# Assigning experts for two of five token tiles during the mixed stage of a transformer layer with a mixture of experts

## The reference, cut to what matters

```python
g_idx   = argmax(softmax(xt @ router_grp_w + router_grp_b))           # 1 of 4 groups
e_logit = (xt @ router_exp_w + router_exp_b).reshape(-1, 4, 4)[.., g_idx]
top_w, top_i = top_k(softmax(e_logit), 2)                             # 2 of its 4 experts
combine = sum(one_hot(g_idx * 4 + top_i) * g_w * top_w / sum(top_w))
out     = sum_e combine[:, e] * (silu(xt @ w_gate[e]) * (xt @ w_up[e])) @ w_down[e]
```

## Time and profile before

| what | value |
|---|---|
| median of 3 runs | 767.57 us (767.41 to 770.96) |
| the profiled execution | 768.89 us |
| its span in the trace | 767.2 us |
| mean granted TensorE clock | 0.974 of full |
| PE, VectorE, ScalarE, GpSimd busy | 714.9, 535.2, 406.7, 108.8 us |

### The profile page before, as it was taken

How to read it: one execution, slowest core, us unless ns; L and a number is a source line. 1 busy time by engine, 2 the same in 40 slices (tenths; PEclk the granted TensorE clock), 3 DMA queues, 4 the chain that set the end, 5 groups by cost and what they waited for, 6 DMA issues and landing times.

```text
span 767.2 us, 10726 instructions
## 1 busy us (share of the span) xinstructions
PE 714.9 (93%) x3858; PEld 538.7 (70%) x3858; DVE 535.2 (70%) x834; ACT 406.7 (53%) x615; POOL 108.8 (14%) x164
## 2 busy tenths in 40 slices
PE   4899999999999989999999389999999999999985
PEld 1359998939989855555554268888888888888753
DVE  5355616369442016667556889999999999999968
ACT  1645523330233015455543467887888878888713
POOL 2000000000031006654221101111111111111000
PEclk9999999999999999999999689999999999999998
DMA  9992235113358649800013899999999999999943
GB/s 323 418 390 109 94 126 220 33 78 124 138 106 213 271 139 398 234 1 30 1 51 131 285 371 387 372 369 385 373 381 392 381 369 379 373 363 366 330 190 137
DMA packets 81905, 188.55 MB, mean 246 GB/s; under 512 B 9092, under 2 KB 19492, under 8 KB 78532
## 3 DMA queue, kind: packets, MB, share of 16 engines
q1 hardware_dynamic: 73652, 168.93, 60.1%
q0 software_dynamic: 6448, 16.86, 6.6%
q10 hardware_dynamic: 1760, 2.17, 0.9%
HBM read 175.46 MB, written 18.38 MB: 253 GB/s over the span
## 4 chain that ended last, share of the span: by engine, by line
PE 86%; DVE 7%; DMA 2%; ACT 2%; issue 1%; SPq 0%; ACTq 0%; POOLq 0%; DVEq 0%
PE bank L1936 55%; PE bank L1838 15%; PE bank L1847 5%; PE bank L1858 3%; PE bank L2087 2%; PE bank L1888 1%; DMA big<-y_scratch 1%; PE bank L2065 1%; PE bank L2058 1%; DVE big L1800 1%; DVE big L1810 1%; DVE big L1256 1%; DVE big L1805 1%; DMA big<-h_scratch,big 1%; PE bank L1873 1%
## 5 line engine op out<-in xcount | busy, mean ns | idle before, releaser
L1651 DVE TENSOR_TENSOR WL<-slot,WH 128x1024 fp32r<-128x1024 f32 x188 | 219.1, 1221 | 9.4 <-ACT WH L1143 8.2
L1143 ACT CAST WH<-slot 128x1024 fp32r<-128x1024 f32 x188 | 183.5, 1057 | 2.4 <-PE bank L1936 1.4
L1936 PE MATMUL bank<-WH,xgTh 128*128 128x512 f32 x256 | 102.4, 400 | 3.0 <-DVE xgTl L1643 3.0
L1936 PE MATMUL bank<-WH,xgTl 128*128 128x512 f32 x256 | 100.7, 393 | 0.0
L1936 PE MATMUL bank<-hTh,WP 128*128 128x384 f32 (+1 forms) x320 | 99.2, 310 | 0.6 <-DVE hTl L1301 0.6
L1936 PE MATMUL bank<-hTh,WL 128*128 128x384 f32 (+1 forms) x320 | 98.7, 308 | 0.0
L1936 PE MATMUL bank<-hTl,WP 128*128 128x384 f32 (+1 forms) x320 | 98.7, 308 | 0.0
L1936 PE MATMUL bank<-WL,xgTh 128*128 128x512 f32 x248 | 96.5, 389 | 0.0
L1838 PE MATMUL bank<-slot,big 128*128 128x512 f32 (+1 forms) x224 | 87.7, 539 | 0.1
L541 DVE TENSOR_TENSOR WL<-slot,WP 128x1024 fp32r<-128x1024 f32 x24 | 29.5, 1247 | 62.0 <-ACT WP L535 61.6
L1847 PE MATMUL bank<-ident,big 128*128 128x128 f32 x424 | 60.9, 284 | 7.5 <-DMA big<-h_scratch,big 5.3
(11 more groups left out here) (265 smaller groups left out, 1079.8 us busy)
## 6 DMA issues: line engine op xcount, KB each, us to landing
slot<-in_w_up SPq DMA_DIRECT2D x16, 2048.0 KB, 17.9
slot<-in_w_down SPq DMA_DIRECT2D x16, 2048.0 KB, 16.7
slot<-in_w_gate SPq DMA_DIRECT2D x15, 2048.0 KB, 15.7
slot<-in_w_ada SPq DMA_DIRECT2D x12, 2048.0 KB, 13.1
slot<-in_w_in SPq DMA_DIRECT2D x6, 2048.0 KB, 18.9
y_scratch<-dftp SPq DMA_DIRECT2D x1, 5120.0 KB, 40.4
big<-y_scratch SPq DMA_DIRECT2D x10, 512.0 KB, 10.2
slot<-in_w_out SPq DMA_DIRECT2D x2, 2048.0 KB, 15.4
```

Source lines behind the costliest of these rows:

```text
L1143: act.copy(WH[:, high_half(w, s), r, :], quarter(n, s, w, r)).then_inc(high_ok[w], 1)
L1651: dve.tensor_tensor(quarter_low(n, s, w, r), quarter(n, s, w, r), WH[:, high_half(w, s), r, :].bitcast(F32), ALU.subtract).then_inc(low_ok ...
L1936: ins = pe.matmul(out, l[u], r[v], start=first and i == 0, stop=last and i == 2)
```

## The change

The code from `first_max` to line 1606 becomes a function `assign(tiles)` on a range of tiles. It is called twice: for tiles 0 and 1 at the end of step 19, behind `weighted` of ("wa", 3, 0), and for tiles 2 to 4 where the code was. PE waits for `assigned` to reach 2 before the ranks. The tables, their places and their numbers stay the same.

```diff
+EARLY_ASSIGNED, EARLY_TILES = 19, 2
...
+            def first_max(val, mx, out, sets):
+
+                n = sets.stop - sets.start
+                link(dve.tensor_reduce(mx[:, sets], val[:, sets], AX, ALU.max))
+                link(dve.tensor_tensor(out[:, sets], val[:, sets], mx[:, sets].broadcast_to([P, n, NG]), ALU.is_equal))
+                link(dve.scalar_tensor_tensor(out=keys[:, sets], in0=out[:, sets], scalar=-float(NG),
+                                              in1=iota[:, 0:NG].unsqueeze(1).broadcast_to([P, n, NG]),
+                                              op0=ALU.mult, op1=ALU.add))
+                link(dve.tensor_reduce(low[:, sets], keys[:, sets], AX, ALU.min))
+                link(dve.tensor_tensor(out[:, sets], keys[:, sets], low[:, sets].broadcast_to([P, n, NG]), ALU.is_equal))
+
+            def assign(tiles):
+
+                sets = slice(tiles.start * SETS, tiles.stop * SETS)
+                first_max(lsets, max1, flat1, sets)
+                link(dve.scalar_tensor_tensor(out=rest_val[:, sets], in0=flat1[:, sets], scalar=-1.0e30, in1=lsets[:, sets],
+                                              op0=ALU.mult, op1=ALU.add))
+                first_max(rest_val, max2, flat2, sets)
+                link(dve.tensor_tensor(by_group(either[:, tiles]), experts1[:, tiles], experts2[:, tiles], ALU.add))
+                dve.tensor_tensor(by_group(A[:, tiles, :]), by_group(either[:, tiles]), in_group(tiles), ALU.mult)\
+                   .then_inc(assigned, 1)
+                n = tiles.stop - tiles.start
+                link(dve.tensor_tensor(by_group(A2[:, tiles]), experts2[:, tiles], in_group(tiles), ALU.mult))
+                link(dve.scalar_tensor_tensor(out=choice[:, 0, tiles], in0=A2[:, tiles], scalar=float(TOK),
+                                              in1=tid[:, tiles].unsqueeze(2).broadcast_to([P, n, NE]),
+                                              op0=ALU.mult, op1=ALU.add))
...
                 if v in LOGITS_AT:
                     logits(LOGITS_AT[v])
+                if v == EARLY_ASSIGNED:
+                    have(dve, "rt", EARLY_TILES - 1)
+                    dve.wait_ge(tm_ok, CT * H)
+                    assign(slice(0, EARLY_TILES))
             have(dve, "rt", NT - 1)
...
-            first_max(lsets, max1, flat1)
-            link(dve.scalar_tensor_tensor(out=rest_val, in0=flat1, scalar=-1.0e30, in1=lsets, op0=ALU.mult, op1=ALU.add))
-            first_max(rest_val, max2, flat2)
...
-            link(dve.tensor_tensor(by_group(either), experts1, experts2, ALU.add))
-            dve.tensor_tensor(by_group(A[:, :, :]), by_group(either), in_group, ALU.mult).then_inc(assigned, 1)
-            link(dve.tensor_tensor(by_group(A2), experts2, in_group, ALU.mult))
+            assign(slice(EARLY_TILES, NT))
...
-            pe.wait_ge(assigned, 1)
+            pe.wait_ge(assigned, 2)
```

More of the change, by code:

```diff
@@ L1520, in weighted, with by_group, in_group @@
                     dve.tensor_tensor(x[:, b, cols], x[:, b, cols], w, ALU.add).then_inc(x1_ok, 1)
+            flat1, flat2 = (v.rearrange("p t g j -> p (t g) j") for v in (first_of, second_of))
+            experts1, experts2 = first_of[:, :, 1:SETS, :], second_of[:, :, 1:SETS, :]
+            def by_group(v):
+                return v.rearrange("p t (g j) -> p t g j", j=EPG)
+            def in_group(tiles):
+                n = tiles.stop - tiles.start
+                return first_of[:, tiles, 0, :].unsqueeze(3).broadcast_to([P, n, NG, EPG])
@@ L1577, in _ @@
                     logits(LOGITS_AT[v])
+                if v == EARLY_ASSIGNED:
+                    have(dve, "rt", EARLY_TILES - 1)
+                    dve.wait_ge(tm_ok, CT * H)
+                    assign(slice(0, EARLY_TILES))
             have(dve, "rt", NT - 1)
[L1580 to L1590, removed]
-            first_max(lsets, max1, flat1)
-            link(dve.scalar_tensor_tensor(out=rest_val, in0=flat1, scalar=-1.0e30, in1=lsets, op0=ALU.mult, op1=ALU.add))
-            first_max(rest_val, max2, flat2)
[L1594 to L1598, removed]
-            link(dve.tensor_tensor(by_group(either), experts1, experts2, ALU.add))
-            dve.tensor_tensor(by_group(A[:, :, :]), by_group(either), in_group, ALU.mult).then_inc(assigned, 1)
-            link(dve.tensor_tensor(by_group(A2), experts2, in_group, ALU.mult))
+            assign(slice(EARLY_TILES, NT))
             def choices(c):
                 return choice[:, c]
-            link(dve.scalar_tensor_tensor(out=choices(0), in0=A2, scalar=float(TOK),
-                                          in1=tid[:, :].unsqueeze(2).broadcast_to([P, NT, NE]), op0=ALU.mult, op1=ALU.add))
             bk = full(dve, "rank")
@@ L1728, in rest_of_routing @@
                 dve.tensor_reduce(e_arg, e_prod, AX, ALU.add).then_inc(route_e, 1)
-                dve.tensor_tensor(by_group(w_first), experts1, in_group, ALU.mult)
+                dve.tensor_tensor(by_group(w_first), experts1, in_group(slice(0, NT)), ALU.mult)
                 low_parts(0, 0, 0, range(1))
```

## The result

| | kernel before | changed kernel |
|---|---|---|
| median, us (lowest to highest of 7 runs each, in turn on one chip) | 767.88 (767.41 to 770.96) | 774.21 (771.22 to 777.24) |
| ratio to before, 95% interval | 1 | 1.0075 [1.0053, 1.0097] |
| profiled execution, its span | 768.89, 767.2 | 774.21, 772.5 |

The change makes the kernel slower by 0.75%. 771.2 had been predicted, with a range that ends at 773.3: the direction was the less likely of the two that were given a real chance, and the size was too small.

A forecast was written before the change was run, and what follows sets the result against it. PE sets the end, with VectorE as critical from 410.04; the first expert's delay counts in full. Lateness +2.55, narrower late part -0.52, clock +1.6 make +3.6 us: 771.2 us on the median, range 768.2 to 773.3.

The forecast's parts named there:

- the block behind 410 moves as one: From `weighted` of ("wa", 3, 1) at 410.04 to 427.67, all moves as a block; its 2.55 us lateness reaches the experts.
- The late part saves 0.52: Behind the last logits, 13 VectorE instructions on three tiles instead of five get shorter: assignments 0.52 us earlier, bounds 0.2 and 0.6.
- The early part costs 3.4 by itself: Fifteen VectorE instructions at step 19 take 3.4 us; the hole swallows 1.9, so `weighted` of ("wa", 3, 1) starts 1.4 late.
- GpSimd's stop adds 1.15: GpSimd's addition of ("wa", 3, 0) halts the early group's second instruction for 1.15 us, making `weighted` of ("wa", 3, 1) 2.55 late.
- Rival (b): GpSimd doesn't stop the early group: lateness and PE's gap about 1.4 us, clock holds, 768.5 us; chance 12%.
- rival (c): VectorE's hole at step 19 holds the whole early group, so only the 0.52 us saving counts: 767.05 us; chance 4%.
- The clock falls: PE stands still 2.6 us, from about 410.8 to 413.4, before tile 2's second turning; its clock then falls to half.
- (a): The clock holds despite PE's 2.6 us gap before the second half of tile 2's turning: 769.6 us; chance 22%.
- It comes back 3.3 us later, and costs 1.6: PE's half clock lasts from about 413.5 to 417 or longer, slowing turning, quarter sums and part of filler ("wa", 4, 0): 1.6 us.
- Rival (d): The low clock stays until filler ("wa", 4, 0) has passed whole, 3.7 us more: 773.3 us; chance 12%.
- the same: The outcome that the changed kernel's time differs from before by under 0.5%, 3.8 us; given 0.59, slower 0.38, faster 0.03.
- the border: The time of 771.4 us above which the changed kernel would count as slower; the forecast was 771.2.

The follow-up runs named there:

- the run without the addition: The changed kernel with GpSimd's addition of ("wa", 3, 0) cut to one of its 512 columns; measured 771.36 us, ratio 1.0034 to the kernel before.
- the early part alone: The changed kernel with its early group kept, but the late code again done for all five tiles as before; measured 775.8 us, ratio 1.0082 to before.

## Why the prediction was wrong

- **What bounds the kernel; the block behind 410 moves as one.** Right. `weighted` late by 2.56 arrives at the ranks undiminished.
- **The late part saves 0.52.** Right: 0.54 in the chain; linked instructions of 60 numbers follow at 0.26 as worked out.
- **The early part costs 3.4 by itself, and GpSimd's stop adds 1.15, so `weighted` is 2.55 late.** Right: 2.56, with a little luck, as the group without the stop took 3.28 and the stop 1.22, and the two misses of 0.1 cancel. Rival (b) (no stop) is refuted by the 1.42 us instruction and by the run without the addition, rival (c) by the second `weighted` directly behind the group, without idle time in front.
- **The clock falls.** Right for the profiles, where (a) is refuted: the gap of 2.53 to 2.54 us was followed by half clock in three of three profiles, those of the changed kernel, its second run and the early part alone. Where the gap was filled or 1.32 us at most, there was none (four kernels, one profile each). But the reason that I gave, that 2.6 us fall and 1.84 don't, came from three gaps in one profile and is no rule: over the 16 profiles the gap of 2.59 was followed by a fall in eleven, that of 1.84 in five. That short work on each side makes a fall likelier, as (a) has it, no run here shows.
- **It comes back 3.3 us later, and costs 1.6.** This is the step that failed: the clock's term of the sum was too small. The clock stayed low for 6.7 us, past the middle of the filler, and cost 0.48 + 2.19 = 2.67 in the table and 2.4 between two kernels on one chip. Rival (d), 3.7 for the whole filler, overshoots by 1.0; the 1.6 fell 1.1 short. I had read the 3.3 off two places of a single profile. The second of them, in the changed kernel, which does the same there:

```profile
288.00:292.00 4.00, 4.00 (x26) 2.94 (x25) 3.28 (x13) 2.57 (x8) 0.86 (x2) 0.50 1.03 415
292.00:296.00 4.00, 4.00 (x21) 2.45 (x18) 1.15 (x4) 1.74 (x6) 2.44 (x5) 0.75 1.04 401
```

and in the profile of before, in the same windows:

```profile
288.00:292.00 4.00, 3.60 (x19) 2.15 (x16) 3.43 (x13) 2.74 (x10) 1.56 (x4) 0.62 1.03 400
292.00:296.00 4.00, 3.85 (x29) 2.50 (x30) 2.01 (x8) 2.04 (x6) 1.16 (x3) 1.00 1.03 413
```

The same fall lasts twice as long in one execution as in the other: 0.50 and 0.75 against 0.62 and 1.00. And the short one is the exception: from 283 to 300 us the mean granted clock is 0.90 in the profile that I had, which is 3.4 us at half clock, and 0.80 in each of the other 15, which is 6.8. "Or longer" stood in the prediction and was not priced. Its reason, PE's waits for ScalarE, isn't borne out: behind 413.61 that wait left PE idle for only about 0.1 us. Why the clock stays low for the longer time is open. With 2.67 for 1.6 the sum is 4.7, and 767.57 + 4.7 = 772.3, inside the range and on the slower side.

- **The chances.** 0.59 stood on "the same" because my number lay 0.2 below the border. The right size of the clock's term alone moves it past. The other 1.9 us of the median of 774.21 are 0.3 by which the median of before moved (767.88 for 767.57) and the open surplus; one profile of each kernel couldn't show them. The range was too tight as well: on its slow side it ended with (d) and left no room for the scatter of times, although the three shown already lay 3.4 apart.

## What to carry to other kernels

A hole in an engine's timeline is free only up to the first instruction behind it that others wait for: add up the new work by the time from one linked start to the next (0.2 to 0.3 us each here, however few the numbers) plus the time for which a neighbour stops them (1.22 us here), and compare it with the hole; the hole one step later, which PE filled itself, took the same 15 instructions at the price of 0.3 us, less than they saved. If the sum spills over and leaves TensorE idle, price the idle time twice, since here 2.5 us of it brought 2.4 us more through the clock. And read from several executions whether the clock falls behind a gap and how long it stays low: one profile showed a fall that five others don't have, and the shorter length of another.

## What the runs showed of the hardware that was not expected

- The low clock behind the gap of about 2.5 us lasted about 7 us in each of the three profiles that had it, though PE was busy almost throughout.
- One and the same gap is followed by a fall of the clock in some executions and not in others, also of one kernel: that of 2.59 us in 11 of 16 profiles, that of 1.84 us in 5 of 16.
- Single executions differ by 3 us in the tail alone (28.4 or 31.4), 1.6 of them taken back in front of it, though the stretch of the kernel before repeats to the hundredth.
- By the records (rough for GpSimd) VectorE's small instruction began 0.06 us ahead of GpSimd's addition and still stood for all of it (1.42 for 0.20 us).
- A one-column memset in a linked row took 0.12 us; a linked instruction of 40 numbers that reads SBUF takes 0.23.
